# The sample's RWKV recurrence moved into the program of the prompt's recurrence

## What is computed

```python
def step(S, inp):
    r_t, w_t, k_t, v_t, kk_t, a_t = inp
    sa = jnp.einsum('bhij,bhj->bhi', S, -kk_t)
    S = (S * w_t[:, :, None, :] + sa[..., None] * (kk_t * a_t)[:, :, None, :]
         + v_t[..., None] * k_t[:, :, None, :])
    y = jnp.einsum('bhij,bhj->bhi', S, r_t)
    return S, y
```

## Time and profile before

| | us |
|---|---|
| median of 3 runs | 4291.13 (4284.9 to 4292.25) |
| the profiled execution, its own time | 4316.1 |
| its span, first to last instruction | 4314.3 |
| TensorE busy in it | 3821.9 (89%) |
| the recurrence's program, first gate product to last, layer 1 | 571.0 to 1079.9 |
| from there to the first DMA of the attention, layer 1 | 1079.9 to 1164.0 |

### The profile page before, as it was taken

One profiled execution on the slowest core, in us unless ns is written; L12 is line 12 of the kernel. 1 busy time (PEld: TensorE's weight loads), 2 busy tenths in 40 slices (PEclk: granted clock), 3 DMA queues, 4 the chain that ended last, 5 costly groups with the idle time before them and its releaser, 6 DMA issues. The chain is left out here.

```text
span 4314.3 us, 66274 instructions
## 1 busy us (share of the span) xinstructions
PE 3821.9 (89%) x28408; PEld 2439.1 (57%) x28408; DVE 1635.8 (38%) x3038; ACT 884.9 (21%) x1772; POOL 254.7 (6%) x277
## 2 busy tenths in 40 slices
PE   5989989999599799989969898999977978999896
PEld 3655656666366555555536555666654655656554
DVE  3021034444367454534122010444534655544422
ACT  1110122221145111111022000222212541112101
POOL 0000000000000222200000000000000012222000
PEclk9999999999699788889989999999987988889897
DMA  7211021111100444433250211111101024443333
GB/s 259 49 41 30 25 52 53 53 52 41 21 13 1 176 158 175 165 116 130 80 189 20 51 35 32 52 51 53 51 24 24 7 87 155 159 176 133 134 120 124
DMA packets 282646, 363.23 MB, mean 84 GB/s; under 512 B 57188, under 2 KB 234294, under 8 KB 265832
## 3 DMA queue, kind: packets, MB, share of 16 engines
q1 hardware_dynamic: 244640, 190.00, 14.9%
q0 software_dynamic: 25808, 155.47, 9.7%
q10 hardware_dynamic: 11896, 13.44, 0.9%
HBM read 310.50 MB, written 48.35 MB: 83 GB/s over the span
## 5 line engine op out<-in xcount | busy, mean ns | idle before, releaser
L842 PE MATMUL rwkv_gate_bank<-u,rwkv_gate_w 128*128 128x364 f32 (+1 forms) x2304 | 789.1, 486 | 8.6 <-DMA rwkv_wa<-in_rwkv_a_dram 8.6
L842 PEld LDWEIGHTS rwkv_gate_bank<-u,rwkv_gate_w 128*128 128x128 f32 x2304 | 420.7, 192 | 233.1 <-issue 11.5
L2170 PE MATMUL dec_s_bank<-u,att_q_rows 32*64 32x256 f32 x8192 | 467.7, 473 | 90.3 <-issue 59.5
L2170 PEld LDWEIGHTS dec_s_bank<-u,att_q_rows 32*64 32x64 f32 x8192 | 286.4, 163 | 236.8 <-issue 193.7
L498 PE MATMUL mla_b<-u,mla_w 128*128 128x364 f32 (+1 forms) x960 | 297.3, 472 | 28.1 <-DMA mla_w<-in_w_in_dram 28.1
L498 PE MATMUL rwp_b<-u,rwp_w 128*128 128x364 f32 (+1 forms) x864 | 266.8, 472 | 3.7 <-DMA rwp_w<-in_w_in_dram 3.7
L498 PEld LDWEIGHTS mla_b<-u,mla_w 128*128 128x128 f32 x960 | 184.1, 192 | 139.6 <-DMA mla_w<-in_w_in_dram 28.2
L2229 DVE STREAM_TRANSPOSE u<-page_ckv 128x2048 f32<-128x2048 f32 x112 | 256.3, 2289 | 0.0
L2464 PE MATMUL out_b<-merged,out_w 128*128 128x364 f32 (+1 forms) x768 | 238.4, 474 | 15.3 <-DMA out_w<-in_w_out_dram 15.3
L498 PE MATMUL conv_b<-u,conv_w 128*128 128x364 f32 (+1 forms) x768 | 238.5, 474 | 5.0 <-DMA conv_w<-in_w_in_dram 5.0
L2194 PE MATMUL dec_o_bank<-page_ckv,cq 128*64 128x256 f32 x1792 | 238.6, 386 | 0.7 <-ACT cq L2221 0.7
(11 more groups left out here) (468 smaller groups left out, 4705.5 us busy)
## 6 DMA issues: line engine op xcount, KB each, us to landing
merge_sig<-gates_feature_major SPq DMA_DIRECT2D x16, 1632.0 KB, 7.8
mod_w<-in_w_ada_dram SPq DMA_DIRECT2D x12, 2048.0 KB, 13.7
rwkv_gate_w<-in_w_in_dram SPq DMA_DIRECT2D x48, 512.0 KB, 4.1
gates_feature_major<-rwkv_gate_stage SPq DMA_DIRECT2D x96, 182.0 KB, 1.9
mla_w<-in_w_in_dram SPq DMA_DIRECT2D x18, 512.0 KB, 3.9
rwp_w<-in_w_in_dram SPq DMA_DIRECT2D x18, 512.0 KB, 4.1
u<-x_feature_major SPq DMA_DIRECT2D x8, 1088.0 KB, 14.1
out_x<-x_feature_major SPq DMA_DIRECT2D x16, 544.0 KB, 5.0
```

Source lines behind the costliest of these rows:

```text
L842: mm = pe.matmul(self.banks[j % 2][:, 0:m], self.w[:, n % GATE_CHUNKS, k, :], self.s.u[:, k, t0:t0 + m], start=(k == 0), stop=(k == KD - 1))
L2170: mm = pe.matmul(S[64 * half:64 * half + NQ, 512 * i:512 * i + NK], q, keys, start=(cb == 0), stop=(cb == BLOCKS))
```

## The change

Programs 2 to 5 become one, `recurrences`. The class `SampleRecurrence` holds the sample's steps for each engine. They stand ahead of the prompt's first block, with 45 gate products between them; the sample's last steps on VectorE (`vector_end`) stand in the prompt's block 0. The states, `wa` and two gate weight chunks are loaded by SyncE behind the projection's weight loads. To have room, the gate weights have 2 buffers and no longer 3, tiles of the prompt serve the sample, and some of the prompt's tiles share memory (`rk` with `kk2`, `ysq` with `b`, `kh` with `pinv`, `kp` with `left`, `u0` with `dv`). A block's head has 23 gate products in place of 26, and the end 11 in place of 24. The new states are turned and copied at the end of the one program and stored by its SyncE part. In the sample's chain the calls of `us` and `y_state` alternate between the two halves of the rows (p innermost), and the new states take 4 products over 128 rows in place of 8 over 64.

```diff
-def project_rwkv(nc, s, l, raw_p, raw_s):
+def project_rwkv(nc, s, l, raw_p, raw_s, load_next):
...
                     pr.load(sp, n, [(0, w_cols(s, l, c))])
+                load_next(sp)
                 dve_s.wait(sp, "out_p")
...
-GATE_CHUNKS = 3
+GATE_CHUNKS = 2
...
-                if n and g == 0:
-                    pe.wait_ge(self.w_in[n % GATE_CHUNKS], 16 * (n // GATE_CHUNKS + (n % GATE_CHUNKS > 0)))
+                if g == 0:
+                    pe.wait_ge(self.w_in[n % GATE_CHUNKS], 16 * (n // GATE_CHUNKS + 1))
                 if j >= 2:
                     pe.wait_ge(self.emptied, j - 1)
...
-        for n in range(1, GATE_CHUNKS):
-            sp.dma_start(self.w[:, n], gate_weights(self.s, l, n)).then_inc(self.w_in[n], 16)
         for j, (n, g) in enumerate(self.jobs):
...
+        fill(2)
+        pe.wait_ge(rows_in, 16)
+        for c in range(2):
+            for b in range(BATCHES):
+                mm = pe.transpose(X[4 + c][:, b * 64:(b + 1) * 64], self.rows[:, b, 2 * c:2 * c + 2, :].rearrange("i h j -> i (h j)"), ident[0:64, 0:64])
+            E.done(mm, f"state{c}")
+        fill(4)
+        pe.wait_ge(wa_in, 32)
+        D.wait(pe, "kk_sq")
+        E.done(pe.matmul(X[1][:, 0:2 * N], s.tab["head_ones"], flat(self.tmp), start=True, stop=True), "kk_norm")
+        A.wait(pe, "tanh")
+        for c in range(2):
+            pe.matmul(X[0][:, c * N:(c + 1) * N], wa[0:64, c * P:(c + 1) * P], self.th, start=True, stop=True)
+        for c in range(2):
+            mm = pe.matmul(X[2][:, c * N:(c + 1) * N], wa[64:P, c * P:(c + 1) * P], mixed[64:P, 6, :], start=True, stop=True)
+        E.done(mm, "lora")
+        fill(13)
+        A.wait(pe, "sig_a")
+        D.wait(pe, "rk")
+        E.done(pe.matmul(X[1][:, 2 * N:4 * N], s.tab["head_ones"], flat(self.tmp), start=True, stop=True), "bonus")
...
+        fill(1)
+        D.wait(pe, "w_t")
+        for b in range(BATCHES):
+            for c in range(2):
+                for p in range(2):
+                    mm = pe.matmul(X[0][par(p), c * N + b * STEPS:c * N + (b + 1) * STEPS], state[par(p), c, b, :], self.w_t[par(p), c, batch(b)],
+                                   start=True, stop=True)
+        E.done(mm, "us")
+        fill(2)
+        D.wait(pe, "us")
+        for c in range(2):
+            mm = pe.transpose(X[2][0:N, c * P:(c + 1) * P], self.u_f[:, c, :], ident)
+        E.done(mm, "u")
+        for b in range(BATCHES):
+            for c in range(2):
+                for p in range(2):
+                    mm = pe.matmul(X[0][par(p), c * N + b * STEPS:c * N + (b + 1) * STEPS], state[par(p), c, b, :], kr[par(p), c, 1, batch(b)],
+                                   start=True, stop=True)
+        E.done(mm, "y_state")
+        fill(2)
+        D.wait(pe, "u")
+        for c in range(2):
+            for p in range(2):
+                h = 2 * p + c
+                out = X[1][par(p), c * N:(c + 1) * N]
+                pe.matmul(out, u[0:N, h, :], ab[p][0:N, c, 1, :], start=True, stop=False, skip_group_check=True)
+                mm = pe.matmul(out, tv[0:N, cols_of(p, c)], dk[p][0:N, c, 1, :], start=False, stop=True, skip_group_check=True)
+        E.done(mm, "y")
+        D.wait(pe, "u_spread")
+        for c in range(2):
+            for p in range(2):
+                mm = pe.matmul(X[4 + c][par(p), 0:512], tbp[:, cols_of(p, c)], self.spread[:, 2 * p + c].rearrange("n b i -> n (b i)"), start=True, stop=True)
+            E.done(mm, f"new_state{c}")
+        fill(3)
+        first_products()
+        fill(2)
+        D.wait(pe, "ys")
+        D.wait(pe, "new_state1")
+        E.done(pe.matmul(X[4][:, 0:2 * N], s.tab["head_ones"], flat(self.y), start=True, stop=True), "mean")
+        fill(3)
+        D.wait(pe, "sq")
+        E.done(pe.matmul(X[4][:, 2 * N:4 * N], s.tab["head_ones"], flat(self.sq), start=True, stop=True), "var")
+
...
-                sp.dma_start(wa[0:64, :], s.ins["rwkv_w2"][l]).then_inc(wa_in, 16)
-                sp.dma_start(wa[64:P, :], s.ins["rwkv_a2"][l]).then_inc(wa_in, 16)
                 gates.move(sp, l)
+                sp.wait_ge(rows_kept, 5)
+                sp.dma_start(s.outs["rwkv_sample"][l].rearrange("b h i j -> i (b h) j"), sample.rows.rearrange("i b h j -> i (b h) j")).then_inc(stored, 16)
+                sp.dma_start(s.outs["rwkv_prompt"][l, 0].rearrange("h i j -> i h j"), row_p.rearrange("i (h j) -> i h j", h=R_HEADS)).then_inc(stored, 16)
+                sp.wait_ge(stored, 32)
...
-                pe.wait_ge(wa_in, 32)
-                fill(8)
-                kk_norm(0)
-                lora(0)
+                def first_products():
+                    kk_norm(0)
+                    lora(0)
+
+                sample.tensor(pe, rows_in, wa_in, first_products)
+                gates.steps = E
                 for i in range(NP):
-                    fill(26)
+                    fill(23)
...
                         lora(i + 1)
                 D.wait(pe, ("y", final))
                 head_sums(final, "mean", A1[:, 0:2 * N], "head_ones", y[final % 2])
-                fill(4)
+                fill()
+                for q in range(2):
+                    sample.turn_back(pe, half(T, q), q, rows_turned)
                 D.wait(pe, ("sq", final))
                 head_sums(final, "var", A0[:, 0:2 * N], "head_ones", ysq)
-                fill()
+                for q in range(2):
+                    sample.turn_back(pe, half(Q, q), 2 + q, rows_turned)
+                for c in range(2):
+                    mm = pe.transpose(A1[0:64, c * P:(c + 1) * P], state[:, at(NP, 0), c, :], ident)
+                mm.then_inc(rows_turned, 1)
...
                 act.wait_ge(eps_set, 1)
-                norm(0)
-                tanh(0)
+                sample.scalar(act, first_norm)
+                sample.scalar_end(act, eps)
...
                 dve.memset(eps[:], 64e-5).then_inc(eps_set, 1)
-                for n in range(3):
-                    mix(0, n)
-                kk_start(0)
+                dve.memset(state[:, 0], 0.0)
+
+                def first_mix():
+                    for n in range(3):
+                        mix(0, n)
+                    kk_start(0)
+
+                sample.vector(dve, rows_in, first_mix)
                 kk_end(0)
...
+                        if i == 0 and m == 8:
+                            sample.vector_end(dve)
...
+                for q in range(2):
+                    sample.keep_row(dve, half(T, q), q, rows_turned, rows_kept)
                 close(final)
-
-
-def rwkv_sample(nc, s, l, raw, state):
-
...
+                for q in range(2):
+                    sample.keep_row(dve, half(Q, q), 2 + q, rows_turned, rows_kept)
+                dve.wait_ge(rows_turned, 5)
+                dve.tensor_copy(row_p, A1[0:64, 0:D_R]).then_inc(rows_kept, 1)
...
+        def load_recurrence(sp):
+            sp.dma_start(row_view, s.ins["state_rwkv"][l].rearrange("b h i j -> i (b h) j")).then_inc(rows_in, 16)
+            sp.dma_start(wa[0:64, :], s.ins["rwkv_w2"][l]).then_inc(wa_in, 16)
+            sp.dma_start(wa[64:P, :], s.ins["rwkv_a2"][l]).then_inc(wa_in, 16)
+            for n in range(GATE_CHUNKS):
+                sp.dma_start(gate_w[:, n], gate_weights(s, l, n)).then_inc(gate_w_in[n], 16)
+
+        project_rwkv(nc, s, l, raw_p, raw_s, load_recurrence)
+        recurrences(nc, s, l, raw_p, raw_s, state_p, state_s, wa, wa_in, rows, rows_in, gate_w, gate_w_in)
```

More of the change, by code:

```diff
@@ L815, with __init__ @@
 class GateFiller:
-    def __init__(self, ph, s, w, banks, steps):
-        self.s, self.w, self.banks, self.steps = s, w, banks, steps
+    def __init__(self, ph, s, w, w_in, banks, orders):
+        self.s, self.w, self.w_in, self.banks, self.orders = s, w, w_in, banks, orders
+        self.steps = orders[0]
         self.ended, self.n_emptied = [], 0
@@ L826, in __init__ @@
         self.stage = [ph.sb(f"gate_stage{i}", [P, THIRD]) for i in range(3)]
-        self.w_in = [ph.sem(f"gate_w_in{i}") for i in range(GATE_CHUNKS)]
         self.multiplied, self.emptied = ph.sem("gate_multiplied"), ph.sem("gate_emptied")
@@ L845, in fill, with empty @@
                 mm.then_inc(self.multiplied, 1)
-                self.ended.append(self.steps.last)
-    def empty(self, act, step=None):
-        before = [e for e in self.ended if step is None or e < self.steps.at[step]]
+                self.ended.append((self.orders.index(self.steps), self.steps.last))
+    def empty(self, act, steps=None, name=None):
+        before = [e for e in self.ended if steps is None or e < (self.orders.index(steps), steps.at[name])]
         for j in range(self.n_emptied, len(before)):
@@ L883, in rwkv_prompt, with recurrences @@
+def recurrences(nc, s, l, raw, raw_s, state, state_s, wa, wa_in, rows, rows_in, gate_w, gate_w_in):
     N, L, HD, NP = RB, CHUNK, R_HEAD, SEQ // RB
@@ L925, in rwkv_prompt @@
         inv, inv_t, below = (ph.sb(n, [P, 4, L]) for n in ("inv", "inv_t", "below"))
```

(38 more changed lines are left out.)

651 lines of the change are left out of this document (276 added, 375 removed).

## The result

| | us |
|---|---|
| before, median of 4 runs | 4291.69 (4284.9 to 4292.72) |
| after, median of 4 runs | 4167.61 (4160.21 to 4174.21) |
| ratio | 0.9714, 95% interval [0.9701, 0.9726] |
| after, the profiled execution | 4160.21 (span 4158.4) |

What follows compares the result with a forecast made beforehand. TensorE's own work bounds the prompt's gate stretch; 96.7 us a layer lie outside. Less 23.1 work, 2.5 waits, 3 clock and 15.5 end, 52.6 us a layer, 105 for both, come off 4291.1: 4186 us, range 4163 to 4228.

Steps and rivals of the forecast that it cites:

- removed: start and end: Per layer, 12.6 us ahead of the first gate product and 84.1 behind the last, outside TensorE's filled stretch: 96.7 us.
- waits: Waits in the sample's part that the 45 gate products do not cover: 2.5 us a layer, bounds 0 and 12.
- clock: TensorE's clock falling between `us` and the new states, small tiles with few gates between: 3 us a layer, bounds 0 to 25.
- the end: From the last gate product to the attention's first DMA: transposes, variance, root, copies, close, store, second barrier: 15.5 us a layer.
- (a): TensorE's 64 `us` instructions, alternating halves of the array at 2.4 GHz: 0.045 us each, 2.9 us in place of 6.5.
- (b): New states, y and y_state on TensorE: 14.8 us at 1.2 GHz become 6.3 by clock, fewer products and alternation.
- (c): The rest of TensorE's small work outside the gate stretch: 21.8 us, at twice the clock 10.9.
- the returns: Returns from a gate group to the sample's chain: some 0.2 us more each, 15 places, 3 us a layer.
- everything fits better: Rival: no wait or clock loss, 20 us of work, a tail of 13; 63.7 us a layer, 4164 us; chance 0.10.
- TensorE did not go cold: Rival: TensorE drops to 1.2 GHz in the sample's part; wholly cold 4274 us, half cold 4230; chance 0.16 for half or more.
- The chain does not show through: Rival: waits of 12 us, not 2.5, from ScalarE's bank copies between its chain steps; 4205 us; chance 0.10.
- The weights are never late: Rival: with 2 buffers gate weights come late, 22 reloads a layer; about 4370 us at 13 us a load; net loss chance 0.02.

Runs made afterwards that it cites:

- exchanged kernel: Changed kernel with the loops of `us` and y_state exchanged, so 32 instructions in a row use one half of the rows: 3905.82 us, ratio 0.9738 to the kernel before.
- bare stretch: Changed kernel with the 5 gate products between `us` and the new states moved ahead of `rk`: 3884.71 us in one execution, beside 4015.65 for the kernel before.
- kernel without cover: Changed kernel without the 45 gate products between the sample's steps, which go to the blocks' heads and the end: 4246.07 us, ratio 0.983 to the kernel before.
- third set: Later runs of the unaltered changed kernel, a version with two edits at its end, and one with loop order exchanged; kernel before 4013.49 us, changed kernel 3885.16.

## Why the prediction was right, and where its terms were off

The direction, the place of the gain and the order of its parts were right: 124 us were measured against 105, inside the range, though 4.6 us above its lower end and just outside the band of small errors (4170 to 4202) that had the chance of 0.60. The terms by layer, as the prediction named them:

| term | forecast | measured |
|---|---|---|
| removed: start and end | 96.7 | 12.7 + 84.1 = 96.8 |
| growth of the gate stretch (work 23.1, waits 2.5, clock 3) | 28.6 | 526.9 - 508.9 = 18.0 |
| the end | 15.5 | 545.6 - 530.4 = 15.2 |
| net | 52.6 | 63.6 |

"Removed" and "the end" held to 0.3 us. The error of 11 us is the middle row alone. Where it lies shows in the first 68.0 us: 68 gate products of 0.61 us are 41.5, which leaves 26.5 for all else, where before 34 products in 29.9 us left 9.2. That is 17.3 of the 18.0. Against the 28.6, step by step:

1. **TensorE's work, (a) and (b): too high by 2.5.** `us`, y_state, y and the new states were put at 2.9 + 6.3 = 9.2 us; they take 2.04 + 2.04 + 1.94 and, for y, 0.66 (598.76 to 599.42), 6.7 in all. The exchange of the halves had been priced at 0.045 us an instruction, after the prompt's groups of 16 (0.039), and in a run of 64 it comes to 0.032. The Trainium skill (TensorE: Matmul & The Clock Gate, section Wait — 56ns, not 53.3ns?) gives a floor of about 25 ns between starts. These rows show 31 to 32 ns at 2.4 GHz, nearer to that floor than to my 45, and not at it. The order of the loops shows its worth in the exchanged kernel: 1.65 to 1.75 us a group, and the clock. The four products over 128 rows in place of eight over 64 were not tested apart.
2. **TensorE's work, (c) and the returns: 2.4 too high.** Some 1.9 of it is a slip: the transposes of the new states and of the prompt's row (3.8 us at 1.2 GHz, so 1.9) were in the 43.1 us of small work and in the end's 15.5 as well. The 2.4 itself is found by subtraction: (c) and the returns were put at 10.9 + 3 = 13.9, and with the measured value of every other term 11.5 are left for them. The other 0.5 has no name.
3. **Waits: 1.3 too high.** 0.77, 0.22, 0.78 and 0.80 less the 1.4 gained at the tanh is 1.2, against 2.5 (the 0.22 is the wait for `dv`; those forecast for `inv_t` and `inv` do not show). No wait came that the prediction had not named.
4. **Clock: 3 too high.** No product of the sample's part behind the first two is cold in the kernel after. The bare stretch shows that the 3 us were no fancy: without the five products the clock falls there, and y_state and the new states take 3.3 us more. So much hangs on the order of the loops, which I had not seen: in the old order the clock falls in spite of the gates. The Trainium skill (same page, section HAM oscillation — how this bites in real kernels), put forward in the prediction as a reason against the change, has waits between bursts of work bring the clock down. The kernel without cover agrees (0.53 over 54 us, with a wait of 8.90), the change does not (0.97).
5. **The cold start: 1.4 too high.** It was to cost what it did, 8 products in 7.5 us, 2.6 above their warm time. Now two are cold (2.44 us, 1.2 above it), and behind the transposes of the states the products are warm.

Together they are the 10.6 missing, 10.1 of it by name. The result comes out at the sum of the rival "everything fits better" (63.7 a layer, 4164 us), which had a chance of 0.10; that rival's own terms (no wait, work of 20, a tail of 13) are not quite what came, and so close a sum is luck. The forecast had five errors of one sign: three cautious values (the small tiles, the waits, the clock), one effect that I had not thought of (the start) and one slip (the transposes). The other rivals fell. TensorE did not go cold. Cold through and through with the gates in it, the case that was priced at 47 us, came up in no run, so its price stays untested; the kernel nearest to it, whose sample part is cold and bare, loses 24.3 us a layer. The chain does not show through: its waits are 1.2 us net, not 12. The weights are never late.

One marker that I named was wrong by its own logic: "the distance of the pairs products, 415.1 us, the same within 3". Three gate products fewer stand at each head, so seven blocks had to be 7 x 3 x 0.61 = 12.8 us shorter. The trace shows 403.4 (625.4 to 1028.8), 11.7 less:

```profile
L1335 PE MATMUL rwkv_q<-rwkv_kr,rwkv_bh x128: 269/269/320, 625.4 to 1028.8; 64*64 64x128 f32 x128
```

Where the 124 us come from, by the runs: taking away the cover loses 51, issuing the loads late 18, the old order of the small tiles 21. Each was taken away alone, with the other two in place, so the three need not add up; if they did, 34 would be left for the program changes, the end and the stores that no longer stand between the steps. No run takes these apart.

## What to carry to other kernels

A chain of small steps that runs alone costs twice, in its waits and in the clock, so look for a neighbour with plain work to lend; here 27 us of gate products lengthened the chain's part by 1.2 us, and a layer lost 24.3 us without them. Issue the next program's loads behind the last weights of this one, and keep two or three products between groups of small tiles: with none, or with runs of 32 instructions on one half of the rows, TensorE fell to 1.2 GHz. When several terms are rounded up for safety, add up the rounding too: here it was over half of the error. And check that no piece of work stands in two terms of the sum.

## What the runs showed of the hardware that was not expected

**The same kernel, 280 us apart in two sets of runs.** The changed kernel takes 4167.61 us in the result and 3885.16 in the third set. The costliest lines of its two traces agree (gate products 792.4 and 793.9 us) but for the page attention's score products. The groups by line in the first:

```profile
L843 PE MATMUL rwkv_gate_bank<-u,rw_gate_w 128*128 128x364 f32 (+1 forms) x2304 | 792.4, 485 | 8.0 <-PEq L171 8.0
L2183 PE MATMUL dec_s_bank<-u,att_q_rows 32*64 32x256 f32 x8192 | 461.2, 481 | 81.2 <-issue 50.6 <-DVE kpe L2245 20.9
```

And in the second:

```profile
L843 PE MATMUL rwkv_gate_bank<-u,rw_gate_w 128*128 128x364 f32 (+1 forms) x2304 | 793.9, 486 | 8.1 <-PEq L171 8.1
L2183 PE MATMUL dec_s_bank<-u,att_q_rows 32*64 32x256 f32 x8192 | 243.8, 384 | 22.5 <-DVE kpe L2245 22.3 <-issue 0.2
```

8192 instructions over 32 rows take 461 us in the one and 244 in the other, with 50.6 us of idle time in "issue" against 0.2. That is 217 us of busy time and 59 of idle time, about the 272 us by which the two spans differ. The kernel before shows the same step: 4319 us on one chip, 4016 and 4013 on two others. So the chip is the likely cause, but no run here tells it from the time at which a set ran, or says what does it. It lies outside the change, whose gain is nearly the same in both (124 and 128 us).

**The clock can fall in one layer and hold in the other, in the same instructions.** In the second trace of the changed kernel, layer 1, the four gate products after the state transposes take 4.23 us in place of 2.71 and the two behind `us` 2.77 in place of 1.49; layer 2 has neither. The first pairs product comes 2.9 us later for it, of which 1.5 are won back at the end (next paragraph): 547.2 us against 545.8. So single us between layers are no finding.

**The same wait does not cost the clock the same.** The wait of 3.17 or 3.18 us for the last `y` is followed by 11 gate products that take 9.40 and 9.38 us in the kernel after, 7.92 and 9.36 in its second trace, 7.91 in both layers of the bare stretch; in the kernel without cover 32 products take 19.63, 0.61 each, with none cold. The prediction had taken 2.4 us as what such a wait costs; these rows have it from nothing to 2.7.
